# Layer 1 MLP of a two-layer diffusion backbone: both products as seven block products from the third pair on, with the weight sums chained in place

## The reference

```python
def _sq_relu_mlp(h, w1, w2):
    return jnp.square(jax.nn.relu(h @ w1)) @ w2      # w1: 1024 x 4096, w2: 4096 x 1024
# in layer i, after the mixer:
h_lat = h_lat + g2 * _sq_relu_mlp(_modulate(_rms_norm(h_lat, norm2_g[i]), sh2, sc2), mlp_w1[i], mlp_w2[i])
```

## Time and profile before

| | us |
|---|---|
| median of 3 runs | 2432.45 (2430.37 to 2434.63) |
| profiled execution: its time is the span | 2428.1 |
| PE busy in the span | 2281.3 (94%) |
| DVE, ACT, POOL busy | 1736.5, 1100.7, 1022.5 |
| layer 1: projection and first pair | 1646.7 to 1798.6 |
| layer 1: one pair of the loop | 40.94 |
| last 19.85 us (output) | PE busy 13.36 |

### The profile page before, as it was taken

One profiled execution on the slowest core, in us unless ns is written; L12 is line 12 of the kernel. 1 busy time (PEld: TensorE's weight loads), 2 busy tenths in 40 slices (PEclk: granted clock), 3 DMA queues, 4 the chain that ended last, 5 costly groups with the idle time before them and its releaser, 6 DMA issues. The chain is left out here.

```text
span 2428.1 us, 36937 instructions
## 1 busy us (share of the span) xinstructions
PE 2281.3 (94%) x11598; PEld 1900.3 (78%) x11598; DVE 1736.5 (72%) x2835; ACT 1100.7 (45%) x1985; POOL 1022.5 (42%) x816
## 2 busy tenths in 40 slices
PE   5989979999999999999699799888999999999998
PEld 3768868888888888888687677766778888888887
DVE  5653787777777777777774688871688787878776
ACT  5553443333333333333443588882343444444443
POOL 0003623433333443333656476765435353545443
PEclk9999999999999999999799899999999999999999
DMA  7434112222222222222212211104111111121212
GB/s 272 176 130 174 66 35 70 86 87 72 84 78 69 70 82 98 69 80 88 105 53 109 81 36 34 35 22 191 44 35 53 51 46 57 37 67 35 69 35 96
DMA packets 79297, 192.75 MB, mean 79 GB/s; under 512 B 6896, under 2 KB 15472, under 8 KB 75888
## 3 DMA queue, kind: packets, MB, share of 16 engines
q1 hardware_dynamic: 76288, 184.92, 22.4%
q10 hardware_dynamic: 2928, 6.82, 0.8%
HBM read 174.94 MB, written 16.78 MB: 79 GB/s over the span
## 5 line engine op out<-in xcount | busy, mean ns | idle before, releaser
L862 POOL TENSOR_TENSOR ht<-ht,l_side 128x512 f32<-128x512 f32 x224 | 301.3, 1345 | 919.2 <-ACT l_side L971 910.8
L1275 DVE SCALAR_TENSOR_TENSOR ht<-l_yy_ps,mod,ht 128x512 f32<-128x512 f32 x672 | 466.1, 743 | 26.9 <-PE l_yy_ps L1591 26.0
L51 PE MATMUL l_z_ps<-nh,l_w1h 128*128 128x512 f32 (+1 forms) x1280 | 474.2, 370 | 11.7 <-DVE nl L1215 6.3
L52 PE MATMUL l_z_ps<-nl,l_w1h 128*128 128x512 f32 (+1 forms) x1280 | 473.2, 370 | 0.0
L53 PE MATMUL l_z_ps<-nh,l_w1l 128*128 128x512 f32 (+1 forms) x1280 | 472.6, 369 | 0.0
L1589 PE MATMUL l_yy_ps<-l_ah,l_w2h 128*128 128x512 f32 x896 | 355.6, 397 | 9.8 <-DVE ht L1275 6.9
L1590 PE MATMUL l_yy_ps<-l_al,l_w2h 128*128 128x512 f32 x896 | 351.0, 392 | 0.0
L1591 PE MATMUL l_yy_ps<-l_ah,l_w2l 128*128 128x512 f32 x896 | 350.5, 391 | 0.0
L971 ACT ACTIVATE l_side<-l_yy_ps,mod 128x512 f32<-128x512 f32 x224 | 154.1, 688 | 335.2 <-PE l_yy_ps L1591 335.2
L51 PEld LDWEIGHTS l_z_ps<-nh,l_w1h 128*128 128x128 f32 x1280 | 242.4, 189 | 54.5 <-issue 7.6
L53 PEld LDWEIGHTS l_z_ps<-nh,l_w1l 128*128 128x128 f32 x1280 | 242.5, 189 | 40.7
(11 more groups left out here) (250 smaller groups left out, 4515.5 us busy)
## 6 DMA issues: line engine op xcount, KB each, us to landing
l_aw<-ada SPq DMA_DIRECT2D x128, 256.0 KB, 2.9
l_w1f<-w SPq DMA_DIRECT2D x64, 512.0 KB, 3.5
l_w2f<-w SPq DMA_DIRECT2D x64, 512.0 KB, 4.9
maw<-ada SPq DMA_DIRECT2D x24, 1024.0 KB, 5.3
queries<-qhl SPq DMA_DIRECT2D x16, 512.0 KB, 2.8
stage<-queries SPq DMA_DIRECT2D x32, 256.0 KB, 2.7
early<-fnet_w SPq DMA_DIRECT2D x11, 512.0 KB, 4.5
early<-wo SPq DMA_DIRECT2D x11, 512.0 KB, 3.5
```

What stands on the lines that cost most here:

```text
L51: pe.matmul(out, lh, rh, start=first, stop=False)
L52: pe.matmul(out, lh, rl, start=False, stop=False)
L862: pool.tensor_tensor(h, h, side[(i - 1) % 2][:], ALU.add).then_inc(s_add, 1)
L1275: dve.scalar_tensor_tensor(out=h, in0=y_ps[m][:], scalar=mod[:, layer, G2, c, 0:1], in1=h, op0=ALU.mult, op1=ALU.add).then_inc(s_acc, 1)
```

## The change

Layer 1's call of `layer_tail` is replaced by a function of its own, `strassen_tail`; layer 0 stays as it is.

- **Pairs 0 and 1** (`PLAIN = 2`) keep the first product in four blocks. The second product's order becomes M1, M6, M7, M4, M5, M3, M2.
- **Tokens.** The norm keeps its results unrounded (`nf`, `t2f`, `t3f`), and in pair 1 sixteen sums on DVE, 16 high parts on ACT and 16 low parts (12 on DVE, 4 on POOL) make the token sums T1 to T4, once for all later pairs. They take the place of blocks of `nh` and `nl` that the plain blocks no longer need.
- **First product from pair 2 on:** seven products M1, M5, M6, M2, M7, M3, M4 of 4 k-steps x 3 matmuls: 84. M1, M6, M7, M4 add up in bank 0, M5 and M3 in bank 2, M2 goes to bank 1. ACT copies M1, M5 and M1+M6 out on the way (`copied`), and DVE makes the blocks B11, B22, B12 from banks and copies (`zsum`), written to banks 1, 3, 2.
- **W1** comes in quarters of 256 KB, four per pair; POOL makes its four sums in place, each from the one before (`sum1`), and the seven low parts (`low1`). DVE makes W2's four sums in place (`sum2`) and three of its low parts, POOL four.
- **Squares:** B11, B12, B22 by DVE, B21 by ACT. Where the block came out negated the sign is taken in the scale. B11, B22, T3 and T4 of the second product stand in the freed banks, B12, B21, T1, T2 in the slots.
- **Deferral:** of a pair's seven second products two (y0, y1) are run at its end, and the other five (y2 to y6) between the seven first products of the next pair. The last pair's five stand alone before the output.
- **Projection:** a third W_o piece buffer besides the two of `early`; three pieces are loaded at once; the first mean is formed one unit earlier.

```diff
-        layer_tail(nc, sem, sb, banks, 1, wo, early, s_pw, w1, w2, mod, meanw, eps, ident, nh, nl, ht, park=park, out=out)
+        strassen_tail(nc, sem, sb, banks, wo, early, s_pw, w1, w2, mod, meanw, eps, ident, nh, nl, nl_at, ht, park, out)
...
+    Z_ORDER = ["M1", "M5", "M6", "M2", "M7", "M3", "M4"]
+    Y_ORDER = ["M1", "M6", "M7", "M4", "M5", "M3", "M2"]
+    TOK_OF = {"M1": "B11", "M2": "B21", "M5": "T1", "M6": "T2", "M3": "B22", "M7": "T3", "M4": "T4"}
+    DEFERRED = 2
...
+            def _(pool):
...
+                def sum1(p, i):
...
+                    if i == 1:
+                        loaded1(pool, p, 1)
+                        loaded1(pool, p, 6)
+                        pool.tensor_tensor(w1f[:, 1], w1f[:, 1], w1f[:, 3], ALU.add).then_inc(s_w1s, 1)
+                    elif i == 2:
+                        pool.wait_ge(s_w1l, w1_at(p, 0))
+                        summed1(pool, p, 1)
+                        pool.tensor_tensor(w1f[:, 0], w1f[:, 0], w1f[:, 1], ALU.add).then_inc(s_w1s, 1)
...
+                def pair(p, more, earlier=True):
+                    low1(p, 3)
+                    sum1(p, 4)
+                    sum1(p, 5)
+                    if earlier:
+                        add(p - 1, 2)
+                    low1(p, 4)
...
+            def _(dve):
...
+                def zsum(p, name):
...
+                    prod, part, k = {"B11": ("M2", "M1", 3), "B12": ("M3", "M6", 1), "B22": ("M7", "M5", 2)}[name]
+                    dve.wait_ge(s_z, z_at(p, prod))
+                    dve.wait_ge(s_cp, copied_at(p, part))
+                    dve.tensor_tensor(z_ps[BANK[name]][:], z_ps[Z_BANK[prod]][:], slot[k][:], ALU.add).then_inc(s_x3, 1)
...
+                def pair_start(p):
...
+                    low(p - 1, "T4")
+                    low(p - 1, "B21")
+                    low(p - 1, "T1")
+                    acc(p - 1, 2)
+                    low(p - 1, "B22")
+                    low2(p - 1, 6)
+                    sum2(p - 1, 5)
+                    acc(p - 1, 3)
+                    low2(p - 1, 5)
+                    acc(p - 1, 4)
...
+                def pair(p, earlier=True):
+                    if earlier:
+                        pair_start(p)
+                    zsum(p, "B11")
+                    if earlier:
+                        acc(p - 1, 5, (0,))
+                    square(p, "B11")
+                    if earlier:
+                        acc(p - 1, 5, (1, 2, 3))
+                    sum2(p, 4)
+                    low2(p, 0)
+                    sum2(p, 1)
+                    sum2(p, 2)
+                    zsum(p, "B22")
+                    square(p, "B22")
+                    zsum(p, "B12")
+                    if earlier:
+                        acc(p - 1, 6, (0,))
+                    square(p, "B12")
+                    if earlier:
+                        acc(p - 1, 6, (1, 2, 3))
+                    low(p, "B11")
+                    diff(p, "T1")
+                    diff(p, "T2")
+                    diff(p, "T3")
+                    low(p, "T2")
+                    acc(p, 0, (0,))
+                    low(p, "T3")
+                    acc(p, 0, (1, 2, 3))
+                    diff(p, "T4")
+                    acc(p, 1)
...
+                sum2(1, 4)
+                low2(1, 0)
+                sum2(1, 1)
+                sum2(1, 2)
+                square(1, "B11")
+                low(1, "B11")
+                for one in (third_sum, first_sum, second_sum, fourth_sum):
+                    for j in range(HK):
+                        one(j)
+                square(1, "B12")
+                square(1, "B22")
+                plain_rest(1)
...
+            def _(pe):
...
+                def pair(p, earlier=True):
+                    behind = {"M1": 2, "M5": 3, "M6": 4, "M2": 5, "M3": 6}
+                    for prod in Z_ORDER:
+                        hidden(p, prod)
+                        if earlier and prod in behind:
+                            product(p - 1, behind[prod])
+                    for i in range(DEFERRED):
+                        product(p, i)
```

957 lines of the change are left out of this document (added).

## The result

The changed kernel takes **2444.84 us** (median of 4 runs, 2443.14 to 2445.83) against 2431.64 (2430.37 to 2434.63) for the kernel before in the same runs: ratio 1.005, 95% interval 1.0036 to 1.0064. It is slower by half a per cent. The forecast was 2420 with a range up to 2441, so the sign and the range are both wrong.

A forecast was written before the change was run, and what follows sets the result against it. The loop was taken as bound by PE's matmul count, DVE next. 38.1 - 3.9 - 0.8 - 12.5 - 1 - 1.9 - 5 = 13.0 us saved, 2432.45 to 2420; own range 2412 to 2428, eighty in a hundred 2405 to 2441.

The forecast's parts named there:

- the walk of a pair: Step-by-step queue timing of one loop pair from M1's start; put y1 from 35.6 against a PE floor of 35.5.
- Removed, 38.1 us: Loop from pair 2: 12 fewer matmuls in each of 14 pairs, 168 x 0.2268 us, saving 38.1 us.
- Loop wait, 0.3 a pair: PE wait in the loop because DVE has no slack: 0.3 us over 13 pairs, 3.9 us lost.
- The walk's other steps: DVE timings from M2's end: 0.6 us per POOL contention, PSUM writes costing 0 extra (bounds 0 to 0.1).
- Before the loop, and pair 0: Stages ahead of pair 0 2.8 us earlier, pair 0's end 3.6 later: net 0.8 us lost.
- Pair 1: Extra DVE token sums and low parts cause 12.5 us of waits, longest 4.8 at y5, plus 1 of half clock.
- Pair 2: No earlier pair's products between its own: waits 0.4 at M4, 1.3 at y0, 0.2 at y1, 1.9 us lost.
- Tail: Last pair's products stand without M1 between: waits 2.1, 1.2 and 1.2 for accumulations, 5 us lost.
- Slower, 2446: Rival: DVE's stretch from M2 to acc1 becomes the loop's bound through POOL meetings, 2.0 us more a pair; chance 0.2.
- PE stays the bound, 2408: Rival: POOL and DVE miss each other in the loop, so its wait is 0 and 24.4 us are saved; chance 0.2.
- A wash: Rival: 0.7 to 1.2 us a pair, or pair 1 loses twice as much: 2428 to 2436; chance 0.12.
- a period above 39.5 (DVE chain): Sign of being wrong: the loop pair's period, expected at 38.2 to 38.8 us, exceeds 39.5 because of DVE's chain.

The follow-up runs named there:

- f1: Changed kernel with, in the loop, DVE's y0 accumulations ahead of low T2, low T3 and diff T3, and ACT's y0 side copy ahead of high T3: 2421.37 us.
- e1: Changed kernel with DVE's accumulations of y0's remaining groups moved ahead of the low part of T3: 2426.64 us, ratio 0.9981 to the kernel before.
- f2: Changed kernel with only DVE's loop order moved: diff T3 early, y0's accumulations around low T2, then low T3: 2422.3 us, ratio 0.9965.
- e4: Changed kernel with POOL's operations of pairs 3 to 14 cut to 4 of 512 columns, order and semaphores unchanged: 2435.13 us, ratio 1.0015.
- e2: Changed kernel with DVE's y0 accumulations ahead of low T2, low T3 and the difference T3, ACT's order unchanged: 2430.42 us, ratio 0.9996.
- e3: Changed kernel with ACT's pair 1 order moved: relu of B22 and high T2, T3 ahead of pair 2's W1 parts: 2441.86 us, ratio 1.0042.
- f3: e3 plus f2's DVE order in pairs 0 and 1, T1's low part behind y5's accumulation, POOL's T2 low parts later: 2442.2 us, ratio 1.0047.
- f4: f3's orders of pairs 0 and 1 together with f2's loop: 2423.43 us, ratio 0.9966 to the kernel before.
- g1: f1's loop together with e3's ACT order in pair 1, the version to keep: 2415.84 us, ratio 0.9935 to the kernel before.

## Why the prediction was wrong

**The step that failed** is in the walk of a pair: "low T2 34.8 [...]: y1 from 35.6", and then "I take 0.3 us of PE wait a pair". It let y1 start as soon as its operand was there and left out its other condition, that y0's accumulation has freed the bank. The walk itself had the numbers. It put the low part of T3 at 37.1 and the accumulation of group 1 one step (0.61) behind, at 37.7; with the 0.80 from a DVE operation to the matmul behind it, y1's group 1 starts at 38.5, where the floor is 35.5 + 0.7 = 36.2. That is 2.3 late, and a period of 38.2 + 2.3 = 40.5. Measured: 40.45. That the two agree to 0.05 is partly luck: in f1, which has no bank wait, the period is 38.65, so the waits and the restarts behind them cost 1.8, not 2.3, and the floor was 0.4 too low. In pairs 0 and 1 I did count the banks ("y1's m0 [...] and m2"); in the loop, where it counts in every pair, I checked only the operands. e1, f1 and f2 show it: the same work in another order gives 39.3, 38.65 and 39.0.

Point by point, in the order of the forecast's sum:

- **Removed, 38.1 us.** Right in count (168 matmuls a pair), but PE's floor of a pair comes out at 38.65 in f1 for 38.2 foreseen. The matmul slot is 100 / 437 = 0.2288 us in f1's stretch for 0.2268; over 168 that is 0.34. Why the slot is 0.002 longer here isn't settled.
- **Loop wait, 0.3 a pair.** Wrong, as above. The 13 periods from y1's end in pair 2 to y1's end in pair 15 take 525.6 us (1885.8 to 2411.3), 28.7 above 13 floors of 38.22, for 3.9 foreseen. This is 24.8 of the 28.2 us between the forecast's span (2415) and the measured one. f1 takes 502.5 for the same stretch, so 23.1 of the 28.7 are the order's, and 5.6 are the longer slot, which no order gave back.
- **The walk's other steps held.** Measured from M2's end, its times on DVE were met to about 0.5 us over 21: the low part of A11 met POOL's add as foreseen (1.77 for 0.69), T4 did too (1.65), and writing a bank costs nothing extra: 0.70 for the bank sum, the figure I took between 0 and 0.1. Contention in that stretch came to 2.0 us on DVE for 1.8 foreseen. By e4 GpSimd's work costs the period 0.7. DVE is busy 35.9 us a pair for 33 to 35 foreseen, POOL 30.9 for 28 to 31.
- **Before the loop, and pair 0: 2.4 us gained for 0.8 lost.** The prediction ends the old pair 0 at 1798.6, and so does the table of times; that is the first matmul of its last group. The last one follows at 1799.05, and pair 1 begins at 1799.28:

```profile
1799.05 0.39 PE L1591 MATMUL l_yy_ps<-l_ah,l_w2l 128*128 128x512 f32 x1
1799.28 0.39 PE L51 MATMUL l_z_ps<-nh,l_w1h 128*128 128x512 f32 x1
```

The changed kernel's pair 0 ends at 1798.76, but its last stage began later. PE's wait for the first low part of W_o, before and after:

```profile
1649.96 0.80 PE L51 MATMUL l_z_ps<-nh,l_ph 128*128 128x512 f32 x1 [7.16 <-DVE l_pl L58]
```
```profile
1651.81 0.79 PE L51 MATMUL l_z_ps<-nh,l_ph 128*128 128x512 f32 x1 [7.14 <-DVE l_pl L58]
```

From there to pair 0's end it is 149.3 us before and 147.0 after. The 1.85 us by which the stages ahead are later in this execution are no work of the change, whose code isn't reached yet; the other versions, all the same up to there, reach this matmul between 1648.9 (e2) and 1653.1 (e3). PE waits 2.00 at the fourth W1 quarter for 2.5 foreseen.
- **Pair 1: 56.9 us for 53 foreseen** (the sum's own terms, 40.94 + 12.5 + 1, give 54.4), 16.0 lost for 13.5. Near in sum, wrong in place. I put 2.2 at y1 and the longest wait, 4.8, at y5. It was 7.13 at y1 and 1.93 at y5. I had followed DVE's queue and not ACT's: relu B22 behind W1's rounding, behind POOL's sum. All waits together are 10.6 for 12.5, and the clock cost more than foreseen: behind PE's idle 7.13 (1823.83 to 1830.96) the granted clock is at the lower of its two levels, 1.2 GHz, and in the whole pair for 10.2 us, which costs about 3.7 us of slots for the 1 I took.

```profile
1828.40:1835.20 6.80, 4.24 (x9) 2.95 (x10) 5.91 (x10) 5.46 (x10) 5.37 (x5) 0.50 0.15 41
```

- **Pair 2: 5.6 lost for 1.9.** M4 waits 1.76 for 0.4, y0 0.96 for 1.3, y1 0.51 and 1.03 for 0.2; these last two are the loop's bank waits again.
- **Tail: 3.4 for 5.** From y1's end in pair 15 to the end it is 31.8 us, with waits of 0.65 and 2.28, restarts, and seven matmuls at the lower clock.

Together 38.1 - 28.7 + 2.4 - 16.0 - 5.6 - 3.4 = 13.2 lost; with the 1.85 by which the last stage began later it is 15.1, and 2443.2 - 2428.1 = 15.1 was measured. The runs' median lies 1.6 above the profiled span, not 4.35 as with the kernel before, which is why the time is off by 25 and the span by 28.

**The rivals.** "Slower, 2446" came within 1.2 us of the time, but by a mechanism that isn't the one at work: it put 2.0 us more a pair on meetings with POOL, of six operations that might meet it two did, and e4 leaves room for 0.7 in all. Its point of decision, 1.3 a pair, was right and was passed. "PE stays the bound, 2408" needed POOL and DVE to miss each other; f1 shows PE can be the bound with every meeting in place, if the bank releases stand early. "A wash" had the sentence that comes nearest to the cause, that DVE has no slack for an ACT that is late, but priced it at 0.7 to 1.2 a pair. The mark I set for being wrong ("a period above 39.5 (DVE chain)") named the right engine.

## What to carry to other kernels

When PE is driven by queues of other engines, list for each matmul group every wait it has, the release of the bank it overwrites beside its operands, and look up where the releasing instruction stands in its engine's queue. An instruction that reads a result bank belongs ahead of anything that may wait for a third engine: here one low part that waited 0.66 us for ACT cost 1.1 us of PE in each pair, and moving it past two accumulations gave 18 us. Moving a producer later to make room (e2, f3) passes the wait to whichever engine reads it next, so walk that queue too before counting the gain. Where a queue holds a long unbroken run of VectorE operations with two SBUF inputs, look for a GpSimd instruction beside it that others wait for: in f4 one was held for the whole run.

## What the runs showed of the hardware

- A VectorE operation that writes a PSUM bank takes as long as one that writes SBUF (0.70 at most against 0.69, both reading a bank), here with GpSimd busy 76% of the time beside it.
- Operations that read a result bank aren't slowed by GpSimd: the accumulations average 0.742 us at POOL 76% busy for 0.743 at 46%, while those with both inputs in SBUF go up to 1.77 in the loop:

```profile
L2547 DVE SCALAR_TENSOR_TENSOR ht<-l_yy_ps,mod,ht 128x512 f32<-128x512 f32 x165 | 116.8, 742 | 1.2 <-PE l_yy_ps L2764 1.1
L58 DVE TENSOR_TENSOR l_w2l<-l_w2f,l_w2h 128x512 fp32r<-128x512 f32 x43 | 62.6, 1456 | 2.3 <-ACT l_w2h L2170 2.3
```

- A GpSimd instruction can be held for more than one VectorE operation. With two SBUF inputs on both sides one took 8.36 us for 1.29 beside twelve operations of VectorE in a row (f4), and 5.37 beside a run of eight (g1); in f3, with f4's instructions up to that place, VectorE gave way instead. What decides which of them gives way wasn't tested.
- DVE at 90% and POOL at 81% busy together still left PE without an idle moment (f1). That GpSimd's work costs only 0.7 us a pair (e4) is what I had not expected. It is the wait at group 0 that goes with it; how the contention brings that wait about wasn't separated.
